# Order of two TensorE stages in the attention loop: weigh the values first, then turn the weights

## The chip, the core and the metric

One core of a Trainium2 chip runs the whole program. The metric is device time in microseconds (us) of one execution; lower is better. Engines are called TensorE (PE in the profile; PEld is its loading of stationary operands), VectorE (DVE), ScalarE (ACT), GpSimd (POOL) and SyncE (SP, which issues most transfers).

## The reference

One decoder layer: a half-step SwiGLU feed-forward block, a mixer of eight forgetting-attention heads (FoX) and eight native-sparse-attention heads (NSA), and a second feed-forward block, for 512 prompt tokens and eight samples of one token each. The part that matters here is the prompt's attention, cut down from the reference:

```python
# FoX heads
s = einsum('bqhd,bkhd->bhqk', q, k) * scale + cum[q] - cum[k]
s = where(kpos <= p, s, NEG)
a = softmax(s, axis=-1)
o = einsum('bhqk,bkhd->bqhd', a, v)
# NSA heads, selected branch and window branch (compressed branch apart)
a_slc, a_win = softmax(masked scores of each branch)
o = g_cmp * o_cmp + g_slc * (a_slc @ v_slc) + g_win * (a_win @ v_win)
```

With 512 tokens every 64-token block that lies before a query is selected, so both NSA branches are causal attention over all earlier keys.

## The kernel before

The feed-forward blocks and the projections (the three-product matmuls of line 1332) keep TensorE busy for most of the time and are not touched. Between them, from 561.8 to 699.6 us of the span, lies the prompt's attention, and behind it, to about 780 us, the attention of the eight samples and the output projection's start.

**Couples.** The attention loop goes over 48 *couples*. A couple is two heads at one block of 128 queries (`unit(v)` for v = 2m and 2m+1; couple m). The block number i = m mod 4 sets how many keys there are: 128·(i+1), so 128, 256, 384, 512 and again. Couples 0 to 15 are FoX heads; from 16 to 47 come the NSA heads, four couples of the selected branch and four of the window branch in turn. Below, *block 3* is a couple with i = 3, the widest.

**The stages of one couple, and who does them:**

- *Scores* (`scores`, lines 1459 to 1467, TensorE): QᵀK for both heads (64 rows of the array each), for FoX the forget sums (line 1465), and the causal mask (line 1467, a bf16 product). Scores of couple m wait for the exponentials of couple m − 2, whose banks they reuse.
- *Row max* (line 1081, VectorE), one instruction for both heads.
- *Exponentials* (line 792, ScalarE), one for each head, each followed by the reading of its accumulated row sum.
- *Scaling* by the reciprocal of the row sum and the gate (line 462), on GpSimd for blocks 0 and 1, on VectorE for blocks 2 and 3.
- *Turn* (`turn_p`, line 1476, TensorE): i+1 transposes for each head into PSUM bank 4 (even head) or 5 (odd head). It waits until that bank's last contents are drained.
- *Drain* (`turn_out`, line 481): VectorE copies the even head's bank, ScalarE the odd head's, into the tile PTS.
- *Weigh* (`weigh`, line 1492, TensorE): PTS times the values, 2(i+1) products of 64 columns, accumulated in bank 6 or 7. It waits for both drains of its couple.

**The order is written out by hand.** In step m TensorE does the scores of couple m, turns couple m − 3 and weighs couple m − 4, in the order that the change is about (function `attention` of the tensor block). Two other engines run the same steps in their own in-order queues. VectorE in step m: drain of couple m − 3 (even head), row max of couple m, reciprocals of couple m − 1, and where due its scaling:

```python
                    if m >= 3 and m != BURST_AT:
                        turn_out(dve, nc.vector.tensor_copy, 2 * (m - 3), "att_even_out")
                    if m < PAIRS:
                        v, W = 2 * m, P * (unit(2 * m)[3] + 1)
                        dve.wait_ge(sem("att_scored"), v + 2)
                        nc.vector.reduce_max(row_max[:, v:v + 2], ...
```

ScalarE in step m: drain of couple m − 3 (odd head), the two exponentials of couple m, and once for each pair of heads a copy of the finished output to OT (line 769). In step 14 (`BURST_AT`) TensorE also runs the 128 products of `windows` (line 1507) between its scores and the rest. Steps 48 to 51 have no scores: they only turn and weigh the last couples. SyncE and GpSimd wait for the last weigh before they start on the samples' part.

Of the kernel before, what the change touches and what calls it, by code (L numbers as in the profile page):

```python
# [122 lines left out]
def of_kind(j, kinds):  # L123

    return sum(t in kinds for t in TILES[:j])
# [7 lines left out]
def unit(v):  # L133

    if v < 4 * HF:
        return True, 2 * (v // 8) + v % 2, 0, v // 2 % 4, v // 8
    w = v - 4 * HF
    return False, 2 * (w // 16) + w % 2, w // 8 % 2, w // 2 % 4, 4 + w // 16
# [32 lines left out]
def layer_kernel(nc, I, O):  # L171
    with ExitStack() as ctx:
        made = {}

        def sem(name):
            if name not in made:
                made[name] = ctx.enter_context(nc.semaphore(name))
            return made[name]
# [1140 lines left out]
        def _(pe):  # L1319
# [130 lines left out]
            def scores(v):  # L1450

                fox, _, br, i, _ = unit(v)
                W = P * (i + 1)
                if v >= 4:
                    pe.wait_ge(sem("att_exp"), v - 2)
                for j in (0, 1):
                    h, part = unit(v + j)[1], slice(64 * j, 64 * j + 64)
                    q, k = (h // 2, h // 2) if fox else (4 + h // 2, 4 + 2 * br + h // 4)
                    nc.tensor.matmul(ps[:, score_bank(v + j), 0:W], QX[part, q, i * P:i * P + P], KX[part, k, 0:W],  # L1459
                                     start=True, stop=False, skip_group_check=True)  # L1460
                for j in (0, 1):
                    h, bank = unit(v + j)[1], ps[:, score_bank(v + j), :]
                    if fox:

                        nc.tensor.matmul(bank[:, 0:W], selb[:, h * P:h * P + P], cumb[:, 0:W],
                                         start=False, stop=False, skip_group_check=True)
                    nc.tensor.matmul(bank[:, W - P:W], identb[:, :], causalb[:, :], start=False, stop=True,  # L1467
                                     skip_group_check=True).then_inc(sem("att_scored"), 1)

            def turn_p(w):  # L1470
                i = unit(w)[3]
                pe.wait_ge(sem(scaled_by(w)), scaled_count(w))
                if w >= 2:
                    pe.wait_ge(sem("att_odd_out" if w % 2 else "att_even_out"), w // 2)
                for kb in range(i + 1):
                    q = nc.tensor.transpose(ps[:, 4 + w % 2, kb * P:kb * P + P],  # L1476
                                            weights(w)[:, kb * P:kb * P + P], ident)
                q.then_inc(sem("att_turned"), 1)

            def weigh(n):  # L1480

                pe.wait_ge(sem("att_even_out"), n + 1)
                pe.wait_ge(sem("att_odd_out"), n + 1)
                fox, _, br, i, t = unit(2 * n)
                first = br == 0 and i == 0
                if first and t >= 2:
                    pe.wait_ge(sem("att_out"), t - 1)
                for kb in range(i + 1):
                    for j in (0, 1):
                        h = unit(2 * n + j)[1]  # L1490
                        c = h * DH if fox else 512 + br * P + (h // 4) * DH
                        q = nc.tensor.matmul(ps[64 * j:64 * j + 64, 6 + t % 2, i * P:i * P + P], VT[:, kb, c:c + DH],  # L1492
                                             PTS[:, (2 * n + j) % PT_SLOTS, kb, :], start=first and kb == 0,
                                             stop=i == QT - 1 and kb == i and (fox or br == 1),
                                             skip_group_check=True)
                q.then_inc(sem("att_pv"), 1)

            def windows():

                for n in (0, 1):  # L1500
                    pe.wait_ge(sem(f"cmp_in{n}"), 16 * (3 + NPAGE))
                pe.wait_ge(sem("att_even_out"), BURST_AT - 3)
                pe.wait_ge(sem("att_odd_out"), BURST_AT - 3)
                for j in range(CMP_LEN):
                    for kv, n in ((0, 0), (1, 1), (0, 1), (1, 0)):
                        r, c = slice(64 * kv, 64 * kv + 64), slice(64 * n, 64 * n + 64)
                        q = nc.tensor.matmul(ps[c, 4 + kv, 0:N_WIN], W1[n][r, j, r],  # L1507
                                             view(X[n][r, :], j, [[CMP_STRIDE, N_WIN]]),
                                             start=j == 0, stop=j == CMP_LEN - 1, skip_group_check=True)
                q.then_inc(sem("cmp_hid"), 1)  # L1510

            def attention():
                for m in range(PAIRS + 4):
                    if m == 16:
                        pe.wait_ge(sem("stack_hi"), of_kind(NPROJ, STACKED))
                        pe.wait_ge(sem("stack_lo"), 2)
                    if m < PAIRS:
                        scores(2 * m)
                    if m == BURST_AT:
                        windows()  # L1520
                        pe.wait_ge(sem("hid_k_out"), 1)
                        pe.wait_ge(sem("hid_v_out"), 1)
                    if 3 <= m < PAIRS + 3:
                        turn_p(2 * (m - 3))
                        turn_p(2 * (m - 3) + 1)
                    if m >= 4:
                        weigh(m - 4)

            project()
            pe.wait_ge(sem("stack_hi"), of_kind(9, STACKED))  # L1530
# [2 lines left out]
            pe.wait_ge(sem("cum_ready"), 1)  # L1533
            pe.wait_ge(sem("bf_ready"), 1)
            attention()


# [277 lines left out]
```

## Time and profile before

| what | value |
|---|---|
| median of 3 runs | 1235.23 us (1234.47 to 1239.1) |
| the profiled execution | 1234.73 us, its span 1232.9 us |
| TensorE busy (PE), loading (PEld) | 1167.1 us (95%), 1078.0 us (87%) |
| VectorE, ScalarE, GpSimd busy | 534.2 us, 429.2 us, 136.0 us |
| chain that ended last, by engine | PE 87%, DVE 6%, ACT 3% |
| scores, L1459 | 192 products, 38.9 us busy |
| weigh, L1492 | 480 products, 36.8 us busy |
| row max, L1081 | 48 instructions, 39.1 us busy |

A row of the timeline reads: start, duration, engine, line, operation, output<-inputs, shapes, count; in square brackets how long the engine was idle before it, and what ended that. Runs of the same kind are merged into one row, so the time from the start of one row to the start of the next is what that stage took of TensorE, and the printed duration is longer by the last product's way through the array.

### The profile page before, as it was taken

How to read it: one execution, taken by the hardware profiler on the slowest of the kernel's cores; microseconds unless marked ns; L12 is line 12 of the kernel's file. 1: busy time of each engine (PE TensorE's matmuls, PEld its weight loads, DVE VectorE, ACT ScalarE, POOL GpSimd, SP SyncE). 2: the span in 40 equal slices, each digit the busy share in tenths (PEclk: the TensorE clock that was granted, in tenths of full speed). 3: DMA queues.
4: the chain of work that ended last, by engine and by line, in shares of the span. 5: the costliest groups of instructions: out<-in, count | busy, mean ns of one | idle time of the engine just before them, and what ended most of it. 6: DMA issues, size and time to landing. Idle time of an engine off the chain costs nothing.

```text
span 1232.9 us, 23635 instructions
## 1 busy us (share of the span) xinstructions
PE 1167.1 (95%) x9643; PEld 1078.0 (87%) x9650; DVE 534.2 (43%) x787; ACT 429.2 (35%) x740; POOL 136.0 (11%) x132
## 2 busy tenths in 40 slices
PE   9999999999999999998999756989999999999994
PEld 6999999999999799995666423979999999999994
DVE  4433432333333743455277646455343333333334
ACT  6222221222234542225266524454222221222332
POOL 0111100010111000223111100210011000011110
PEclk9999999999999999999999988999999999999998
DMA  6322223322223133217060062121232223222221
GB/s 273 103 75 95 86 78 111 103 84 87 78 87 111 54 121 135 90 62 236 20 205 2 7 185 103 68 69 47 91 102 80 69 100 114 83 102 89 66 86 70
DMA packets 46002, 117.95 MB, mean 96 GB/s; under 512 B 4154, under 2 KB 21818, under 8 KB 39874
## 3 DMA queue, kind: packets, MB, share of 16 engines
q1 hardware_dynamic: 42738, 110.95, 26.8%
q10 hardware_dynamic: 3184, 5.88, 1.2%
q8 instruction: 58, 0.95, 0.3%
q14 instruction: 22, 0.18, 0.0%
HBM read 110.93 MB, written 7.97 MB: 96 GB/s over the span
## 4 chain that ended last, share of the span: by engine, by line
PE 87%; DVE 6%; ACT 3%; issue 2%; DMA 1%; DVEq 0%; SPq 0%; ACTq 0%
PE ps L1332 75%; PE ps L1459 3%; PE ps L1476 2%; PE ps L1341 1%; PE ps L1507 1%; PE ps L1492 1%; DVE row_max L1081 1%; DVE UT L919 1%; DVE H L923 1%; DVE XL L899 1%; PE ps L1467 1%; ACT PRB L792 1%; PE ps L1425 0%; DMA RAW<-in_w_gu 0%; DMA KW<-in_win_k 0%
## 5 line engine op out<-in xcount | busy, mean ns | idle before, releaser
L1332 PE MATMUL ps<-XH,WH 128*128 128x260 f32 x1904 | 389.9, 286 | 8.0 <-DVE XL L899 7.9
L1332 PE MATMUL ps<-XH,WL 128*128 128x260 f32 x1904 | 383.7, 283 | 0.0
L1332 PE MATMUL ps<-XL,WH 128*128 128x260 f32 x1904 | 383.0, 283 | 0.0
L409 ACT CAST WH<-RAW 128x1024 fp32r<-128x1024 f32 (+2 forms) x183 | 174.8, 956 | 530.8 <-PE ps L1332 526.2
L1332 PEld LDWEIGHTS ps<-XH,WH 128*128 128x128 f32 x1904 | 295.2, 189 | 14.2 <-DVE XL L899 11.3
L1332 PEld LDWEIGHTS ps<-XH,WL 128*128 128x128 f32 x1904 | 293.7, 189 | 0.0
L1332 PEld LDWEIGHTS ps<-XL,WH 128*128 128x128 f32 x1904 | 293.1, 188 | 0.0
L412 DVE TENSOR_TENSOR WL<-RAW,WH 128x1024 fp32r<-128x1024 f32 (+2 forms) x183 | 203.7, 1113 | 157.9 <-ACT WH L409 156.7
L1332 PE MATMUL ps<-UL,WH 128*128 128x260 f32 x704 | 141.9, 283 | 0.0
L1332 PE MATMUL ps<-UH,WL 128*128 128x260 f32 x704 | 141.5, 282 | 0.0
L1332 PE MATMUL ps<-UH,WH 128*128 128x260 f32 x704 | 141.4, 282 | 0.0
L1277 POOL TENSOR_TENSOR UL<-HT,UH 128x520 f32 (+1 forms) x44 | 57.8, 1314 | 632.8 <-ACT UH L665 632.8
L1332 PEld LDWEIGHTS ps<-UH,WL 128*128 128x128 f32 x704 | 108.5, 188 | 0.0
L1332 PEld LDWEIGHTS ps<-UH,WH 128*128 128x128 f32 x704 | 108.4, 188 | 0.0
L1332 PEld LDWEIGHTS ps<-UL,WH 128*128 128x128 f32 x704 | 108.3, 188 | 0.0
L939 DVE TENSOR_TENSOR UT<-ps,token_rstd 128x520 f32<-128x520 f32 x44 | 30.8, 700 | 145.8 <-PE ps L1332 145.8
L935 DVE TENSOR_TENSOR GT<-ps,token_rstd 128x520 f32<-128x520 f32 x44 | 30.8, 700 | 128.7 <-PE ps L1332 119.9
L665 ACT CAST UH<-HT 128x520 f32 (+1 forms) x44 | 27.6, 627 | 86.0 <-DVE HT L946 86.0
L1052 DVE TENSOR_TENSOR TR<-ps,token_rstd 128x520 f32<-128x520 f32 x23 | 16.1, 700 | 67.9 <-PE ps L1332 44.8
L1459 PE MATMUL ps<-KX,QX 64*128 64x128 f32 (+3 forms) x192 | 38.9, 481 | 6.5 <-ACT PRB L792 5.1
L1081 DVE TENSOR_REDUCE row_max<-ps 128x2 f32<-128x256 f32 (+3 forms) x48 | 39.1, 815 | 6.7 <-PE ps L1467 6.7
L1270 POOL TENSOR_TENSOR ACC<-ACC,SQ 128x520 f32<-128x520 f32 x18 | 27.0, 1501 | 96.1 <-ACT SQ L613 96.1
(233 smaller groups left out, 927.4 us busy)
## 6 DMA issues: line engine op xcount, KB each, us to landing
RAW<-in_w_gu SPq DMA_DIRECT2D x44, 1024.0 KB, 4.8
RAW<-in_w_down SPq DMA_DIRECT2D x16, 768.0 KB, 4.7
RAW<-in_w_in SPq DMA_DIRECT2D x11, 1024.0 KB, 4.9
RAW<-in_w_down SPq DMA_DIRECT2D x16, 640.0 KB, 4.3
KF<-in_fox_k SPq DMA_DIRECT2D x16, 256.0 KB, 4.2
VF<-in_fox_v SPq DMA_DIRECT2D x16, 256.0 KB, 5.1
RAW<-in_w_out SPq DMA_DIRECT2D x4, 1024.0 KB, 4.9
H<-in_x SPq DMA_DIRECT2D x4, 520.0 KB, 7.2
```

Source lines behind the costliest of these rows:

```text
L409: nc.scalar.copy(WH[:, par, 0:width], RAW[:, slot, j, 0:width]).then_inc(w_hi, 1)
L412: nc.vector.tensor_tensor(WL[:, par, 0:width], RAW[:, slot, j, 0:width], WH[:, par, 0:width], ALU.subtract).then_inc(w_lo, 1)
L665: nc.scalar.copy(row(UH, st.m), HT[:, st.par, :]).then_inc(sem("hid_hi"), 1)
L935: nc.vector.tensor_tensor(two(GT[:, st.par, :]), halves(0), two(R1[:, :]), ALU.mult).then_inc(sem("evac"), 1)
L939: nc.vector.tensor_tensor(two(UT[:, st.par, :]), halves(1), two(R1[:, :]), ALU.mult).then_inc(sem("evac"), 1)
L1052: nc.vector.tensor_tensor(two(TR[:, j % 4, :]), halves(j % 2), two(R1[:, :]), ALU.mult).then_inc(sem("projected"), 1)
L1081: nc.vector.reduce_max(row_max[:, v:v + 2], ps[:, score_bank(v):score_bank(v) + 2, 0:W], AX.X, negate=True).then_inc(sem("att_max"), 1)
L1270: nc.gpsimd.tensor_tensor(ACC[:, :], ACC[:, :], SQ[:, par, :], ALU.add).then_inc(sem("acc"), 1)
L1277: nc.gpsimd.tensor_tensor(row(UL, st.m), HT[:, st.par, :], row(UH, st.m), ALU.subtract).then_inc(sem("hid_lo"), 1)
L1332: q = nc.tensor.matmul(ps[:, 2 * slot + half, 0:HALF], w[:, par, cols], x[:, kt0 + kt, half * HALF:(half + 1) * HALF], start=first and kt ...
L1459: nc.tensor.matmul(ps[:, score_bank(v + j), 0:W], QX[part, q, i * P:i * P + P], KX[part, k, 0:W], start=True, stop=False, skip_group_check ...
L1476: q = nc.tensor.transpose(ps[:, 4 + w % 2, kb * P:kb * P + P], weights(w)[:, kb * P:kb * P + P], ident)
```

## The change

In every step of the tensor block's attention loop the weigh of couple m − 4 is issued before the turns of couple m − 3, not behind them. Nothing else differs: the same instructions, waits and signals, on the other engines in the same order.

```diff
@@ -1520,11 +1520,11 @@
                         windows()
                         pe.wait_ge(sem("hid_k_out"), 1)
                         pe.wait_ge(sem("hid_v_out"), 1)
+                    if m >= 4:
+                        weigh(m - 4)
                     if 3 <= m < PAIRS + 3:
                         turn_p(2 * (m - 3))
                         turn_p(2 * (m - 3) + 1)
-                    if m >= 4:
-                        weigh(m - 4)
```

TensorE around a block-3 step, the two orders in one (L1459 and L1467 are scores, L1476 turns, L1492 weighs; a row's shape is its output):

```order
 L1459 MATMUL ps<-KX,QX 128x512 x2
 L1467 MATMUL ps<-causalb,identb 128x128 x2
+L1492 MATMUL ps<-PTS,VT 64x128 x8
 L1476 MATMUL ps<-consts,PRA 128x128 x2
-L1492 MATMUL ps<-PTS,VT 64x128 x8
 L1459 MATMUL ps<-KX,QX 128x128 x2
 L1467 MATMUL ps<-causalb,identb 128x128 x2
+L1492 MATMUL ps<-PTS,VT 64x128 x2
 L1476 MATMUL ps<-consts,PRA 128x128 x4
-L1492 MATMUL ps<-PTS,VT 64x128 x2
```

The weigh now stands directly behind the scores, and the turns directly ahead of the next scores.

TensorE at the loop's end, from the scores of couple 47 (steps 47 to 51), again both in one:

```order
 L1459 MATMUL ps<-KX,QX 128x512 x2
 L1467 MATMUL ps<-causalb,identb 128x128 x2
+L1492 MATMUL ps<-PTS,VT 64x128 x8
 L1476 MATMUL ps<-consts,PRA 128x128 x2
+L1492 MATMUL ps<-PTS,VT 64x128 x2
+L1476 MATMUL ps<-consts,PRA 128x128 x4
+L1492 MATMUL ps<-PTS,VT 64x128 x4
+L1476 MATMUL ps<-consts,PRB 128x128 x6
+L1492 MATMUL ps<-PTS,VT 64x128 x6
+L1476 MATMUL ps<-consts,PRB 128x128 x8
 L1492 MATMUL ps<-PTS,VT 64x128 x8
-L1476 MATMUL ps<-consts,PRA 128x128 x4
-L1492 MATMUL ps<-PTS,VT 64x128 x2
-L1476 MATMUL ps<-consts,PRB 128x128 x6
-L1492 MATMUL ps<-PTS,VT 64x128 x4
```

Here each weigh now follows at once on the turns of its own couple; before, the turns of the next couple stood between them.

VectorE in the block-3 step and the one behind it, the same before and after the change:

```order
L481 COPY PTS<-ps 128x128
L1081 TENSOR_REDUCE row_max<-ps 128x2
L1086 RECIPROCAL row_inv<-row_sum 128x2
L462 TENSOR_SCALAR PRB<-PRB,row_inv,gates 128x384 x2
L481 COPY PTS<-ps 128x256
L1081 TENSOR_REDUCE row_max<-ps 128x2
```

The drain of the couple turned in a step (L481) stands ahead of the row max (L1081) of the couple scored in that step.

## Rows read from the trace of the kernel before

**Rows 1.** Busy time in two stretches (columns PE, PEld, DVE, ACT, POOL, PEclk, DMA share, GB/s).

```profile
613.60:699.60 86.00, 81.28 (x775) 52.87 (x776) 62.71 (x152) 53.66 (x175) 15.91 (x32) 1.00 0.25 81
560.00:570.00 10.00, 7.53 (x54) 4.07 (x55) 4.67 (x11) 6.27 (x19) 3.39 (x5) 1.00 0.89 316
```

**Rows 2.** Timeline of TensorE over four steps, scores of block 3 first.

```profile
653.13 1.13 PE L1459 MATMUL ps<-KX,QX 64*128 64x512 f32 x4
654.20 0.29 PE L1467 MATMUL ps<-causalb,identb 128*128 128x128 bf16 x2
654.32 0.39 PE L1476 MATMUL ps<-consts,PRA 128*128 128x128 f32 x2
654.64 1.09 PE L1492 MATMUL ps<-PTS,VT 128*64 128x128 f32 x16
655.66 0.49 PE L1459 MATMUL ps<-KX,QX 64*128 64x128 f32 x4
...
657.59 0.70 PE L1459 MATMUL ps<-KX,QX 64*128 64x256 f32 x4 [0.41 <-ACT PRB L792]
...
658.35 0.82 PE L1476 MATMUL ps<-consts,PRB 128*128 128x128 f32 x6
659.10 0.66 PE L1492 MATMUL ps<-PTS,VT 128*64 128x128 f32 x8
659.69 0.92 PE L1459 MATMUL ps<-KX,QX 64*128 64x384 f32 x4
...
660.66 1.04 PE L1476 MATMUL ps<-consts,PRB 128*128 128x128 f32 x8
661.64 0.88 PE L1492 MATMUL ps<-PTS,VT 128*64 128x128 f32 x12
662.44 1.13 PE L1459 MATMUL ps<-KX,QX 64*128 64x512 f32 x4
...
664.97 0.49 PE L1459 MATMUL ps<-KX,QX 64*128 64x128 f32 x4
```

**Rows 3.** Timeline of the same stretch, VectorE and ScalarE.

```profile
654.64 0.29 DVE L481 COPY PTS<-ps 128x128 f32<-128x128 f32 x1 [1.01 <-PE ps L1476]
...
654.84 1.21 DVE L1081 TENSOR_REDUCE row_max<-ps 128x2 f32<-128x1024 f32 x1
...
656.09 0.69 ACT L792 ACTIVATE PRB<-ps,row_max 128x512 f32<-128x512 f32 x1 [1.08 <-DVE row_max L1081]
...
657.34 0.20 ACT L792 ACTIVATION_READ_ACCUMULATOR PRB<-ps,row_max 128x1 f32 x1
...
663.93 0.20 ACT L792 ACTIVATION_READ_ACCUMULATOR PRB<-ps,row_max 128x1 f32 x1
```

**Rows 4.** Waits from 560 to 725 us: total us, times, longest.

```profile
PE ps L1459 <- ACT PRB L792: 5.1, 12, 0.8
```

**Rows 5.** Timeline, scores of couple 0 to scores of couple 1.

```profile
562.45 0.22 PE L1467 MATMUL ps<-causalb,identb 128*128 128x128 bf16 x1
562.60 0.70 PE L1459 MATMUL ps<-KX,QX 64*128 64x256 f32 x4
```

**Rows 6.** Timeline of the loop's end.

```profile
694.66 0.37 ACT L481 COPY PTS<-ps 128x256 f32<-128x256 f32 x1
...
694.74 0.95 PE L1476 MATMUL ps<-consts,PRB 128*128 128x128 f32 x6 [0.83 <-DVE PTS L481]
...
695.73 0.48 ACT L481 COPY PTS<-ps 128x384 f32<-128x384 f32 x1 [0.70 <-PE ps L1476]
...
696.62 1.06 PE L1476 MATMUL ps<-consts,PRB 128*128 128x128 f32 x8 [0.33 <-DVE PTS L481]
...
697.72 0.59 ACT L481 COPY PTS<-ps 128x512 f32<-128x512 f32 x1 [1.51 <-PE ps L1476]
...
699.58 0.59 ACT L769 COPY OT<-ps 128x512 f32<-128x512 f32 x1 [1.27 <-PE ps L1492]
```

## The prediction

> **What bounds the kernel now.** I read the busy time by stretch first. From 613.6 us to the loop's end TensorE is busy 81.28 of 86 us at a granted clock of 1.00, VectorE, the next, 62.71 of 86 [rows 1]. So time on TensorE is time of the kernel, and the question is what TensorE waits for. The table of waits names one thing inside the loop: scores wait for the exponentials of a wide couple, 12 times, 5.1 us in all [rows 4]. The timeline of four steps shows where: only the scores of a block-1 couple stop, by 0.41 us, and what releases them is the exponential (PRB, L792) of the block-3 couple two steps earlier [rows 2]. The other three steps of the four run without a stop.
>
> That wait ends a chain that I follow with the third view [rows 2, 3]. Scores of block 3 start at 653.13, the turns behind them at 654.32. VectorE drains the even head at 654.64 as soon as its turn is there, having been idle for 1.01 us, and only then, at 654.84, takes the row max of the scores, which had been ready since about 654.49 (654.20 + 0.29). The row max lasts 1.21 us, the exponentials run from 656.09 to 657.54 (657.34 + 0.20), and the scores of couple m + 2 start at 657.59. The chain takes 657.59 - 653.13 = 4.46 us; TensorE's own work in the same two steps is 4.46 - 0.41 = 4.05 us. **The reader should see one thing in these rows:** the row max stands behind the drain in VectorE's queue, the drain waits for the turn, and so the turn is on the chain while the weigh, which comes after it, is not. TensorE's products run beside VectorE's row max.
>
> **The change, part by part.** Nothing is added or removed; in each step that has both, the weigh moves ahead of the turns; 44 of these steps have scores too. No transfer and no instruction of another queue moves.
>
> *The block-3 step.* With the weigh between scores and turns, the drain starts later by the whole weigh, and with it row max, exponentials and the scores of couple m + 2. The weigh of a block-3 couple takes 654.64 to 655.66 = 1.02 us of TensorE [rows 2]. Since the scores already wait there, nothing absorbs it.
>
> *What a switch costs.* The products of a stage start on one another closely, but where the shape of the loaded operand changes there is a step. From the masks of the scores to the turns, both 128 by 128, two masks and the switch take 654.20 to 654.32, 0.06 us for each mask [rows 2]. From the last mask to the next scores, 64 rows instead of 128, it is 562.45 to 562.60 = 0.15 us [rows 5]. The new switch from masks to a weigh (64 columns) is in no row of the loop. I bound it by these two: 0.00 to 0.09 us more than the switch that it replaces, and I take 0.09, since the weigh is a change of shape too. The other two switches, weigh to turns and turns to scores, take the place of weigh to scores and turns to weigh, all four with a change of shape, so I put their difference at nothing.
>
> The chain becomes 4.46 + 1.02 + 0.09 = 5.57 us, TensorE's work in it 4.05 + 0.18 = 4.23 us, the wait 1.34 us in place of 0.41. It is paid for the block-3 couples 7, 11, ..., 43, which is 10 times (couple 3 has no weigh in its step, couple 47 belongs to the end): 10 x 1.11 = **11.1 us**.
>
> *The Trainium skill on this switch.* "TensorE: Matmul & The Clock Gate", section "Step-by-step: what each phase is for", says that the engine can pull the loading of the next operand ahead of products in flight. By that the weigh's first load hides behind the masks, the 0.09 is 0, and the sum is the 1247.0 worked out under the rivals; the pair of rows that I go by speaks against it for a change of rows, and no row shows it for a change of columns.
>
> *The other steps.* Blocks 1 and 2 stay bound by TensorE and pay only the switch. Of the 44 steps 20 lie in the ten chains, step 47 in the end, step 4 disappears in a wait, step 14 has the compression products between scores and weigh: 21 x 0.09 = **1.9 us**. Do their chains have room? The nearest is block 2: scores start at 659.69, exponentials end at 664.13 (663.93 + 0.20), the scores that need them start at 664.97, so 0.84 us are left [rows 2, 3]. The weigh of block 2 adds 0.80 (661.64 to 662.44) and a switch 0.09, and TensorE itself comes 0.18 later: 0.84 - 0.89 + 0.18 = 0.13 us are left. Just enough, so I cost it at nothing; if this cover fails it is paid ten times.
>
> *The loop's end.* Behind the last scores each weigh now waits for ScalarE's drain of turns issued just before it. Couple 45's drain ends at 695.03 (694.66 + 0.37); it stands behind the exponentials of couple 47, whose chain is 1.11 longer, so 696.14, and the weigh starts at 696.19. From there, with stage lengths from the rows: weigh 45 0.59 (659.10 to 659.69), turns 46 0.75 (658.35 to 659.10), a wait, weigh 46 0.80, turns 47 0.98 (660.66 to 661.64), a wait, weigh 47 1.02 [rows 2]. A wait is ScalarE's drain, 0.48 and 0.59, and 0.16 around it (0.07 until the turn's printed end, 0.04 and 0.05 for the two signals): 0.64 and 0.75 [rows 6]. In sum 701.72, and with 0.11 until the last product is out 701.83, against 699.58 now: **2.2 us**. The two waits that turns have there today, 0.83 and 0.33, are already inside the 699.58.
>
> *Sum.* 11.1 + 1.9 + 2.2 = 15.2 us. Everything behind the loop waits for its last weigh and moves as a whole. On the profiled execution: 1234.73 + 15.2 = 1249.9, rounded to **1250**; that execution lies 0.5 us below the median of the three runs, far less than 0.5% of the time (6.2 us), which is about what a measurement of this kernel can tell from no change.
>
> **The rivals.**
>
> *The switch is free* (0.20). Chain and end alone: 10 x 1.02 + 2.1 = 12.3, so 1247.0. For it: masks to turns shows none. Against it: the change of shape.
>
> *The block-2 chain binds too, or a scaling comes late* (0.10). The 0.13 us of room is a difference of larger numbers. If drains or scalings cost 0.1 to 0.4 more than I think, ten periods pay 1 to 4 us: 1251 to 1254.
>
> *Turns gain what scores lose, and the kernel is faster* (0.02). A turn waits until its bank is drained; behind the weigh the drain has more time. If the scores' wait were made by the turns and not by the row max behind the drain, all 5.1 us of it [rows 4] and the 0.83 + 0.33 at the end [rows 6] could go: 1234.7 - 6.3 = 1228.4. It decides itself at the drain: were VectorE busy until the turn is done, the row max would lose nothing. Against it: VectorE was idle 1.01 us ahead of that drain [rows 3]. The skill's "Perfetto Trace Analysis", section "Matmuls", asks that groups rotate through banks so that copying one out overlaps the next group's products. By that rule the new order is the better one, with the weigh between two uses of the turn's banks; the trace shows no wait for these banks inside the four steps, so the rule has nothing to win there.
>
> *The extra delay is hidden* (0.05). If the exponentials had other work to wait for, only the end and the switches would stay, 0 to 4 us: 1235 to 1239. Against it: ScalarE was idle for 1.08 us until the row max came [rows 3].
>
> *The granted clock falls to the lower of its two levels* (0.03), because TensorE now waits more: its 8.9 us of work in four steps would take about twice as long, 8.9 us for each time: 1259 and more. Against it: from 560 to 570 us TensorE was busy only 7.53 of 10 us at a granted clock of 1.00 [rows 1], and the new loop would be about 87% busy.
>
> **How the numbers follow.** The forecast has 0.60 and gives 1250. The range takes in the free switch (1247.0) and the binding block 2 (1254), and 1 to 2 us at either side for the runs: 1245 to 1255. Outside lie the last three rivals, together 0.10, and the tails of the others, so about 0.15. Faster by over 0.5%: 0.02. Within 0.5% (1229 to 1241.4): 0.05. Slower by over 0.5%: 0.93.
>
> **What would show it.** Right, step by step: scores of block 1 wait 1.2 to 1.4 us for the exponential of block 3, where it was 0.41; four steps of NSA heads take 10.6 us where they take 9.31 (653.13 to 662.44); the weigh starts 0.15 us behind the last mask (0.06 if the switch is free); row max of block 3 starts 1.1 us later after its scores; in the loop's end weighs wait for drains and turns do not; behind the loop all is as it was. Wrong: scores of block 1 with a wait of 0.4 us or none, a wait at the scores of block 0, or a granted clock under 1.00 before 700 us.

## The result, and the profile after

The changed kernel takes 1261.26 us (median of 4 executions, 1259.64 to 1264.59) where the kernel before, on the same chips, took 1237.16 us: a ratio of 1.020, 95% interval 1.018 to 1.022. A second measurement later in the study gave 1261.75 against 1236.94 us, ratio 1.020, interval 1.018 to 1.022. So the change costs 24 to 25 us. It was forecast to be slower, but by 15 us, and the time lies above the range.

The page of the profiled execution (1264.59 us, span 1262.7 us) shows the same work in a longer span. Its first part gives busy time, its second the granted clock in 40 slices, in tenths of full speed:

```profile
PE 1186.0 (94%) x9643; PEld 1087.8 (86%) x9650; DVE 533.1 (42%) x787; ACT 430.0 (34%) x740; POOL 136.0 (11%) x132
...
PEclk9999999999999899999999867999999999999997
```

VectorE and ScalarE do as much as before. TensorE is busy 19 us longer with the same products. About 6 us of that are the dearer switches between stages that the experiments price (44 steps at 0.145 us, an estimate from their rows); the rest are products that ran slower: the mean granted clock is 0.966, where it was 0.983.

Four steps of NSA heads on TensorE, answering to [rows 2]; the columns are those of that group:

```profile
654.67 1.13 PE L1459 MATMUL ps<-KX,QX 64*128 64x512 f32 x4
655.74 0.29 PE L1467 MATMUL ps<-causalb,identb 128*128 128x128 bf16 x2
655.95 1.09 PE L1492 MATMUL ps<-PTS,VT 128*64 128x128 f32 x16
656.98 0.44 PE L1476 MATMUL ps<-consts,PRA 128*128 128x128 f32 x2
657.34 0.49 PE L1459 MATMUL ps<-KX,QX 64*128 64x128 f32 x4
...
660.30 0.70 PE L1459 MATMUL ps<-KX,QX 64*128 64x256 f32 x4 [1.29 <-ACT PRB L792]
...
665.43 1.13 PE L1459 MATMUL ps<-KX,QX 64*128 64x512 f32 x4
```

From block 3 to block 3 it is 10.76 us instead of 9.31, and the scores of block 1 wait 1.29 us instead of 0.41. VectorE and ScalarE in the same stretch, answering to [rows 3]:

```profile
657.34 0.29 DVE L481 COPY PTS<-ps 128x128 f32<-128x128 f32 x1 [1.37 <-PE ps L1476]
...
657.55 1.22 DVE L1081 TENSOR_REDUCE row_max<-ps 128x2 f32<-128x1024 f32 x1
...
658.80 0.69 ACT L792 ACTIVATE PRB<-ps,row_max 128x512 f32<-128x512 f32 x1 [1.08 <-PE ps L1476]
...
660.05 0.20 ACT L792 ACTIVATION_READ_ACCUMULATOR PRB<-ps,row_max 128x1 f32 x1
```

The scores of block 3 start at 654.67 and the row max at 657.55, 2.88 us later; it was 1.71 (653.13 to 654.84). The drain in front of the row max came 1.17 us later because its turn stood behind the weigh. That is the forecast mechanism, and 1.1 was the forecast size.

What was not in the forecast is the granted clock. Busy time by stretch (PE, PEld, DVE, ACT, POOL, then PEclk), three stretches inside the loop and two around its end:

```profile
671.00:681.80 10.80, 9.47 (x84) 5.87 (x84) 7.00 (x17) 6.07 (x22) 1.99 (x4) 1.00 0.00 0
681.80:685.20 3.40, 3.38 (x20) 2.30 (x20) 1.50 (x5) 1.45 (x6) 0.00 (x0) 0.57 0.03 7
685.20:696.00 10.80, 9.51 (x85) 5.85 (x84) 6.65 (x16) 6.03 (x20) 1.99 (x4) 0.98 0.00 0
704.80:716.00 11.20, 8.96 (x80) 5.58 (x81) 7.15 (x18) 6.75 (x22) 1.99 (x4) 1.00 0.01 1
716.00:726.00 10.00, 7.55 (x50) 5.84 (x50) 4.72 (x25) 2.03 (x4) 0.96 (x2) 0.52 0.00 1
```

From 681.8 to 685.2 us, in the middle of the loop, the mean granted clock is 0.57: most of this stretch lies at the lower of TensorE's two levels (1.2 instead of 2.4 GHz). From 716 us on it is there again. Before the first of these it had been waiting 1.29 us of every 10.76; before the second it had waited 0.45 and 1.77 us for two drains. The loop's end on TensorE, answering to [rows 6]:

```profile
713.15 0.44 PE L1492 MATMUL ps<-PTS,VT 128*64 128x128 f32 x4 [0.45 <-ACT PTS L481]
...
715.94 0.72 PE L1492 MATMUL ps<-PTS,VT 128*64 128x128 f32 x8 [1.77 <-ACT PTS L481]
...
718.79 1.55 PE L1492 MATMUL ps<-PTS,VT 128*64 128x128 f32 x12 [0.66 <-ACT PTS L481]
...
723.01 1.97 PE L1492 MATMUL ps<-PTS,VT 128*64 128x128 f32 x16 [0.77 <-ACT PTS L481]
...
725.02 0.59 ACT L769 COPY OT<-ps 128x512 f32<-128x512 f32 x1 [2.15 <-PE ps L1492]
```

The waits are the forecast ones (0.66 and 0.77 for couples 46 and 47; 0.64 and 0.75 were worked out), but the weighs at 718.79 and 723.01 run at half speed, 1.55 and 1.97 us for what takes 0.88 and 1.09.

Where the time went in one profiled execution of each kernel. The program is cut at the first and the last scores, at the last copy to OT (L769) and at the output projection's first product; us:

```
                        until    first to   to the    to the    rest   mean
                        first    last       last      output           granted
                        scores   scores     OT copy   proj.            clock
before                  561.85   128.51      9.22     69.38    463.94  0.983
changed                 563.70   146.26     15.06     73.79    463.89  0.966
changed, again          561.82   148.03     11.90     74.27    463.88  0.970
old order at the end    562.78   146.51     11.44     73.80    463.87  0.970
new order, block 3      560.62   142.93     10.39     69.38    463.98  0.982
new order, not block 3  562.77   131.85      9.21     70.22    463.95  0.980
changed, idle products  562.46   146.30     11.90     70.16    463.98  0.979
changed, row max first  561.67   131.13     10.71     72.16    463.83  0.979
before, row max first   560.83   127.60      8.90     69.33    463.94  0.982
new order at the end    561.79   128.82     10.73     74.21    463.85  0.974
before, long delay      561.02   149.69     12.99     71.87    463.93  0.973
before, short delay     560.98   141.72     11.41     74.16    463.93  0.973
before, both first      561.07   137.57      9.49     73.80    463.87  0.975
```

The first column is the same code in all of them, so its 3 us of spread are not the change's.

One thing in this table needs care: the only profile of the kernel before is of one of its faster executions. Its 25 executions in the second measurement fall into two groups, 13 at 1233.9 to 1236.9 us with a granted clock of 0.980 to 0.984, and 12 at 1238.0 to 1240.3 us with 0.974 to 0.979.

### The profile page after: what moved, and what is told of

It is laid out like the page before. It is cut to its first block, busy times and chain, and to the rows that moved or that the text cites. A ratio compares the mean times of both kernels' runs of the same rounds, so it can differ in the third digit from the quotient of the medians.

```text
span 1262.7 us, 23635 instructions
## 1 busy us (share of the span) xinstructions
PE 1186.0 (94%) x9643; PEld 1087.8 (86%) x9650; DVE 533.1 (42%) x787; ACT 430.0 (34%) x740; POOL 136.0 (11%) x132
## 4 chain that ended last, share of the span: by engine, by line
PE 89%; DVE 5%; ACT 3%; issue 2%; DMA 1%; DVEq 0%; SPq 0%; ACTq 0%
PE ps L1332 74%; PE ps L1459 3%; PE ps L1492 3%; PE ps L1476 3%; PE ps L1341 2%; PE ps L1507 1%; DVE UT L919 1%; ACT PRB L792 1%; DVE H L923 1%; PE ps L1467 1%; DVE XL L899 1%; DMA RAW<-in_w_gu 1%; PE ps L1634 0%; PE ps L1425 0%; DMA KW<-in_win_k 0%
## 5 line engine op out<-in xcount | busy, mean ns | idle before, releaser
L1459 PE MATMUL ps<-KX,QX 64*128 64x128 f32 (+3 forms) x192 | 40.3, 497 | 15.2 <-ACT PRB L792 13.8
L481 DVE COPY PTS<-ps 128x128 f32<-128x128 f32 (+3 forms) x48 | 23.5, 489 | 52.3 <-PE ps L1476 52.3
L1492 PE MATMUL ps<-PTS,VT 128*64 128x128 f32 x480 | 38.9, 294 | 4.5 <-ACT PTS L481 3.6
```

The lines of the kernel that those rows point to most:

```text
L481: copy(PTS[:, w % PT_SLOTS, 0:i + 1, :], ps[:, 4 + w % 2, 0:P * (i + 1)].rearrange("p (a n) -> p a n", n=P)).then_inc(sem(name), 1)
```

## The experiments

Each edit is against the kernel before, unless it says otherwise; where only the line with `weigh_first` is shown, the other lines are those of the first edit. Two theories. **The queue:** TensorE waits longer because the drain stands ahead of the row max on VectorE, and the granted clock falls because TensorE waits. **The order itself:** the changes of operand shape, or the weighs' own waits, make the cost, and the clock falls for the new order or by chance. "m" is the step; PAIRS is 48.

### The end in the old order

```diff
+                    weigh_first = m < PAIRS
-                    if m >= 4:
+                    if m >= 4 and weigh_first:
                         weigh(m - 4)
                     if 3 <= m < PAIRS + 3:
                         turn_p(2 * (m - 3))
                         turn_p(2 * (m - 3) + 1)
+                    if m >= 4 and not weigh_first:
+                        weigh(m - 4)
```

> The new order in steps 4 to 47, the old one in steps 48 to 51. If the chain through the row max makes the loop's cost and the waits of the last weighs make the rest (directly, and through the lower granted clock behind them), this is 15 to 18 us over the kernel before, the clock behind the loop is as before (about 0.8), and the stretch from the last weigh to the output projection's first product is back at 69 to 71 us. If the clock falls because of the waits inside the loop, little changes: 21 to 24 us over, and that stretch stays at 73 to 74 us.

Measured: 1259.61 us against 1238.41, ratio 1.017, interval 1.014 to 1.021, so 21 us over. The clock is 0.970 and the stretch to the output projection stays at 73.80 us. It is the second case: against the changed kernel the old end saves 2 to 4 us (by the medians, or by the differences to the kernel before), and the clock does not need the waits of the last weighs to fall.

### The new order in the block-3 steps alone

```diff
+                    weigh_first = m < PAIRS and m % 4 == 3
```

> The new order only in the steps that score a block-3 couple (one of four). Chain theory: scores of block 1 wait about 1.3 us and four steps take 1.1 to 1.2 us more than before, 11 to 13 us in all. If instead the changes of operand shape in every step make the cost, only a quarter of it is here: 3 to 5 us in all, and the wait stays near 0.4 us.

Measured: 1250.40 us against 1238.41, ratio 1.012, interval 1.008 to 1.015: 12 us. On TensorE:

```profile
646.34 0.70 PE L1459 MATMUL ps<-KX,QX 64*128 64x256 f32 x4 [1.43 <-ACT PRB L792]
...
652.25 0.28 PE L1467 MATMUL ps<-causalb,identb 128*128 128x128 bf16 x2
652.46 1.09 PE L1492 MATMUL ps<-PTS,VT 128*64 128x128 f32 x16
653.49 0.44 PE L1476 MATMUL ps<-consts,PRA 128*128 128x128 f32 x2
653.86 0.49 PE L1459 MATMUL ps<-KX,QX 64*128 64x128 f32 x4
...
656.81 0.70 PE L1459 MATMUL ps<-KX,QX 64*128 64x256 f32 x4 [1.43 <-ACT PRB L792]
```

Four steps take 10.47 us, 1.16 more than before, from one step of four. The chain holds. The rows also give the switches: masks to weigh 0.21 us (652.25 to 652.46) where masks to turns were 0.12, so 0.09 dearer, as taken; weigh to turns 1.03 for 1.02; but from the first turn to the next scores 0.37 (653.49 to 653.86) where from the first turn to the weigh it was 0.32. That 0.05 had been put at nothing. Where it arises, single rows show. The kernel before (PE products, PEld loads):

```profile
654.26 0.22 PE L1467 MATMUL ps<-causalb,identb 128*128 128x128 bf16 x1
654.26 0.20 PEld L1476 LDWEIGHTS ps<-consts,PRA 128*128 128x128 f32 x2
654.43 0.27 PE L1476 MATMUL ps<-consts,PRA 128*128 128x128 f32 x1
```

The changed kernel:

```profile
655.80 0.22 PE L1467 MATMUL ps<-causalb,identb 128*128 128x128 bf16 x1
655.95 0.85 PEld L1492 LDWEIGHTS ps<-PTS,VT 128*64 128x64 f32 x16
656.98 0.33 PE L1476 MATMUL ps<-consts,PRA 128*128 128x128 f32 x1
657.14 0.27 PE L1476 MATMUL ps<-consts,PRA 128*128 128x128 f32 x1
```

The second turn starts 0.16 us behind the first (656.98 to 657.14), where it was 0.11 (654.32 [rows 2] to 654.43). From the second turn to what follows it is the same, 0.20 (657.14 to 657.34) and 0.21 (654.43 to 654.64). So the 0.05 lies in the first turn, which now stands behind a stage of another shape, and it is on the chain: 1.02 + 0.09 + 0.05 = 1.16.

### The new order everywhere but in the block-3 steps

```diff
+                    weigh_first = m < PAIRS and m % 4 != 3
```

> The new order in all steps with scores but those of block 3. Chain theory: the three short chains have room, so only the switches are paid, 1 to 4 us over the kernel before, and the wait of the block-1 scores stays at 0.4 us or less. If every weigh ahead of a turn is on a chain, 6 us or more.

Measured: 1239.44 us against 1238.41, ratio 1.002, interval 1.000 to 1.004. Three quarters of the change cost 1 us by the medians (the interval allows 0 to 4), and 3.3 us of loop in the profile:

```profile
646.65 1.13 PE L1459 MATMUL ps<-KX,QX 64*128 64x512 f32 x4
...
651.11 0.70 PE L1459 MATMUL ps<-KX,QX 64*128 64x256 f32 x4 [0.24 <-ACT PRB L792]
...
656.25 1.13 PE L1459 MATMUL ps<-KX,QX 64*128 64x512 f32 x4
```

Four steps take 9.60 us, 0.29 more than before, and 0.29 + 1.16 is the whole 1.45 of the changed kernel. The two parts add up.

### Idle products in the waits of the end

Added to the changed kernel:

```diff
+WARM_END = {49: 8, 50: 3, 51: 3}
...
                     if m >= 4:
+                        if m in WARM_END:
+                            pe.wait_ge(sem("att_exp"), 94)
+                            keep_warm(WARM_END[m], bank=0)
                         weigh(m - 4)
```

> The changed kernel with 14 idle products (512 columns, bf16, result never read) put into the waits of the last three weighs, 8, 3 and 3 of them, 0.2 us each at the full clock. If the lower granted clock in the last turns and weighs comes from TensorE standing still there, those stages run at 1.00, the loop's end takes 11 to 12 us instead of 15, and the kernel is 4 to 8 us faster than the changed one. If the clock falls for another reason, the products only add: no faster, or 1 to 3 us slower than the changed kernel.

Measured: 1260.21 us against 1238.41, ratio 1.019, interval 1.016 to 1.023, about 1 us less than the changed kernel and far from 4 to 8. The end took 11.90 us, as expected, but in the changed kernel's second profile it took 11.90 too, without the products. The stretch behind it was 70.16 us in this profile, where it was 73.79 and 74.27; with a median as high as it is, that can't be put down to the products. The attempt failed. In this profile two stretches at the lower level lie inside the loop, at 636 and 681 us, ahead of these products, which can do nothing about them.

### The changed kernel with the row max ahead of the drain

```diff
                 for m in range(PAIRS + 3):
-                    if m >= 3 and m != BURST_AT:
-                        turn_out(dve, nc.vector.tensor_copy, 2 * (m - 3), "att_even_out")
                     if m < PAIRS:
...
                                              negate=True).then_inc(sem("att_max"), 1)
+                    if m >= 3 and m != BURST_AT:
+                        turn_out(dve, nc.vector.tensor_copy, 2 * (m - 3), "att_even_out")
```

> The changed kernel with VectorE's queue turned round in each step: row max first, then the drain. If the cost comes over the drain that stands ahead of the row max, the weigh is off the chain again, the scores of block 1 wait 0.2 us or less, four steps take 9.5 to 9.8 us, the granted clock is as in the kernel before, and the whole is 3 to 7 us over it. If the cost lies in the order on TensorE itself (switches of shape, waits for the drains), it stays 15 us or more over.

Measured: 1241.22 us against 1236.94, ratio 1.004, interval 1.002 to 1.005: 4 us over. TensorE's order is the changed one, instruction by instruction, and 20 of the 24 us are gone:

```profile
649.34 0.70 PE L1459 MATMUL ps<-KX,QX 64*128 64x256 f32 x4
...
654.48 1.13 PE L1459 MATMUL ps<-KX,QX 64*128 64x512 f32 x4
...
658.92 0.70 PE L1459 MATMUL ps<-KX,QX 64*128 64x256 f32 x4
```

The scores of block 1 are down to 0.11 us of idle time (the views print only what is over 0.15), four steps take 9.58 us, and no stretch of the loop is at the lower level. This decides for the queue. What is left in the loop is the switches: 9.58 against the 9.00 of the next kernel, where the same queue meets the old order, is 4 times 0.145 us.

### The kernel before with the row max ahead of the drain

The same edit of VectorE's queue, made to the kernel before.

> The kernel before with the same turn in VectorE's queue, the order of TensorE as it was. Chain theory: the 0.41 us wait of the block-1 scores, 11 times, goes to under 0.1 us and the loop is 3 to 4.5 us shorter, so 3 to 4 us faster than the kernel before. If drains that now come later stop the turns or the weighs, no gain or a loss of 1 to 3 us.

Measured: 1232.36 us (8 executions, 1230.59 to 1234.52) against 1236.94, ratio 0.9964, interval 0.9949 to 0.9979. **It beats both kernels**, by 4.6 and 29 us. The block-3 step there, all three engines:

```profile
653.51 0.28 PE L1467 MATMUL ps<-causalb,identb 128*128 128x128 bf16 x2
653.63 0.39 PE L1476 MATMUL ps<-consts,PRA 128*128 128x128 f32 x2
653.84 1.22 DVE L1079 TENSOR_REDUCE row_max<-ps 128x2 f32<-128x1024 f32 x1 [1.34 <-PE ps L1467]
...
654.98 0.28 DVE L481 COPY PTS<-ps 128x128 f32<-128x128 f32 x1
...
655.09 0.69 ACT L792 ACTIVATE PRB<-ps,row_max 128x512 f32<-128x512 f32 x1 [0.77 <-DVE row_max L1079]
```

The row max now starts 0.33 us behind the start of the masks (653.51 to 653.84) and no longer waits for the turn. In the same timeline TensorE is idle for 0.10 us ahead of the scores of block 1, where it was 0.41, so this chain has almost gone; four steps take 9.00 us (647.60 to 656.60 in the same timeline). The drain comes later and holds nobody up inside the loop.

### The new order at the end alone

```diff
+                    weigh_first = m >= PAIRS
```

> The new order in steps 48 to 51 only. The loop is as before; its end takes about 1.1 us longer at the full clock. If the longer waits there are enough to bring the granted clock down, the turns and weighs behind them take about 3 us more and the stretch to the output projection 3 to 4 more: 6 to 8 us over the kernel before. If the waits inside the loop are needed for that too, 1 to 3 us over.

Measured: 1240.66 us against 1236.94, ratio 1.003, interval 1.001 to 1.004: 3.7 us, between the two cases. The end takes 10.73 us, 1.5 more than before (1.1 was worked out). In the profile the stretch behind it takes 74.21 us instead of 69.38, but the clock of its ten executions, 0.971 to 0.979, overlaps that of the kernel before (0.974 to 0.984 in the 25 executions beside it). But not one of the ten lies in the upper group, 0.980 and more, where 13 of those 25 do. So a few waits at the end can cost some clock, 2 us by the medians, but not the 7 us in question.

### The changed kernel again

> The changed kernel once more, beside the others on one chip. If the lower granted clock is part of the change and not of one execution, its share is again 0.966 to 0.975, with stretches at the lower level inside the loop, at its end and behind it, and the time is 22 to 25 us over the kernel before; if it was chance, 16 to 18 us over at a clock of 0.98.

Measured: 1261.75 us (1260.79 to 1262.59), 24.8 us over, with a granted clock of 0.969 to 0.972 in all four executions. The lower clock belongs to the change. In this profile the loop has three stretches at the lower level (at 625, 659 and 703 us), in the first it had two (at 566 and 682 us), and the loop was 1.8 us longer.

### A delay in place of the new order

TensorE keeps its old order; VectorE does further row maxes whose results nobody reads, ahead of the real one (`unread` is a new tile). The short delay has WIDTHS = (512,).

```diff
+WIDTHS = (512, 128)
...
                         dve.wait_ge(sem("att_scored"), v + 2)
+                        if m >= 4 and m % 4 == 3:
+                            for e, n in enumerate(WIDTHS):
+                                c = 4 * (m // 4) + 2 * e
+                                nc.vector.reduce_max(unread[:, c:c + 2],
+                                                     ps[:, score_bank(v):score_bank(v) + 2, 0:n], AX.X,
+                                                     negate=True)
```

> TensorE in its old order; the block-3 row max is made later by two further row maxes of the same scores (512 and 128 columns), whose results nobody reads. The chain grows by about 1.13 + 0.34 = 1.47 us, as much as four steps of the changed kernel take more, so that TensorE waits 1.9 us for each block-1 scores: 11 x 1.47 = 16 us from the waits. If waits alone bring the granted clock down inside the loop, as in the changed kernel, its share is 0.970 to 0.976 and the kernel is 20 to 24 us over the one before; if the new order of TensorE is needed for that, the clock stays at 0.98 and it is 15 to 18 us over.

Measured: 1261.12 us against 1239.05, ratio 1.018, interval 1.016 to 1.020: 22 us, with a clock of 0.969 to 0.974. Four steps at the full clock took 10.76 us, to the hundredth what the changed kernel takes. In the timeline (lines are shifted by 8 in this kernel, so L1467 is scores) and by stretch:

```profile
670.47 0.70 PE L1467 MATMUL ps<-KX,QX 64*128 64x256 f32 x4 [1.87 <-ACT PRB L794]
...
673.21 1.65 PE L1467 MATMUL ps<-KX,QX 64*128 64x384 f32 x4
...
682.76 0.70 PE L1467 MATMUL ps<-KX,QX 64*128 64x256 f32 x4 [1.87 <-ACT PRB L794]
```

```profile
670.50:677.00 6.50, 6.50 (x48) 4.10 (x50) 3.67 (x9) 3.00 (x11) 0.88 (x2) 0.74 0.01 1
677.00:681.00 4.00, 3.89 (x38) 2.26 (x38) 2.99 (x6) 1.42 (x5) 1.09 (x2) 1.00 0.02 4
```

Behind a wait of 1.87 us the scores of block 2 take 1.65 us instead of 0.92, and this period lasts 12.29. The old order on TensorE, with nothing but longer waits, gives the same time and the same clock as the changed kernel. So the waits bring the clock down, not the new order. The added work on VectorE is no rival for that: it is busy 549.0 us here, but 533.1 in the changed kernel, as before.

> The same with the wide further row max alone: the chain grows by 1.13 us, as it did where only the block-3 steps had the new order. 11 x 1.13 = 12.4 us over the kernel before, four steps of NSA heads in 10.4 us, no lower clock inside the loop.

Measured: 1254.39 us against 1239.05, ratio 1.012, interval 1.010 to 1.015: 15 us, where 12.4 was expected. Four steps took 10.44 us as worked out (645.65 to 656.09 in its timeline), but there was one stretch at the lower level inside the loop, and the clock was 0.971 to 0.977.

### Exponentials ahead of the drain as well

On top of the row max first, ScalarE does both exponentials of couple m before the drain of couple m − 3:

```diff
-                    if m >= 3 and m != BURST_AT:
-                        turn_out(act, nc.scalar.copy, 2 * (m - 3) + 1, "att_odd_out")
                     if m < PAIRS:
                         act.wait_ge(sem("att_max"), m + 1)
...
                                 sem("att_exp"), 1)
+                    if m >= 3 and m != BURST_AT:
+                        turn_out(act, nc.scalar.copy, 2 * (m - 3) + 1, "att_odd_out")
```

> The kernel before with row max ahead of the drain on VectorE and both exponentials ahead of the drain on ScalarE. The chain through the row max is as short as it gets, but ScalarE's drain of couple m - 3 comes 1 us and more later, and the odd head's next turn waits for it: where the wait of the block-1 scores has gone, waits of the odd turns after block-3 and block-2 exponentials come in its place. 0 to 8 us slower than the kernel with the row max alone moved; if nothing waits for those drains it is the same within 1 us.

Measured: 1248.26 us against 1239.05, ratio 1.008, interval 1.006 to 1.010. It is 14 to 16 us slower than the row max alone (by the differences to the kernel before, or by the medians), about twice what was allowed for. The wait has moved:

```profile
652.88 0.26 ACT L481 COPY PTS<-ps 128x128 f32<-128x128 f32 x1
...
653.29 0.41 PE L1476 MATMUL ps<-consts,PRA 128*128 128x128 f32 x2 [0.93 <-ACT PTS L481]
```

The drain of the block-0 couple now stands behind both exponentials of block 3, and the odd head's next turn waits 0.93 us for it. Four steps take 9.96 us (644.04 to 654.00). The same trade that pays on VectorE loses on ScalarE, whose work between turn and drain is longer.

## Why the prediction was wrong

**The bound and the chain: right.** The row max behind the drain behind the turn was named as the chain, and the weigh as what would be put on it. The block-3 steps alone cost 1.16 us for four steps (1.11 was worked out), three quarters of the change cost next to nothing, and with the row max moved ahead of the drain the cost went, TensorE's order unchanged. That is shown by runs on both sides: the order without the cost, and the cost (by a delay) without the order.

**The switches: mis-sized, 0.145 for 0.09.** Masks to weigh cost 0.09 more, as taken from the pair of rows on a change of rows; the rival of a free switch (0.20) falls. The Trainium skill, "TensorE: Matmul & The Clock Gate", section "Step-by-step: what each phase is for", says that the engine can pull a load ahead of products in flight, under conditions. The trace agrees for the turns in the kernel before, whose first load starts with the last mask (654.26 and 654.26), and not for the weigh in the changed kernel, whose first load starts 0.15 us behind the last mask (655.95 and 655.80). What the prediction left out is that the first turn behind the weigh is 0.05 us slower; the other switches differ by nothing in their starts, as it had put them. So a step pays 0.145 (0.58 for four steps) where 0.09 was counted. Masks, turns and weighs differ in more than the shape of the loaded operand, and no run separates the shape from the rest. At the full clock the ten periods cost 14.5 us (10.76 - 9.31 = 1.45 each) and the loop, with two more dear switches in its last steps, about 14.8; the prediction had 11.1 + 1.9 = 13.0.

**The cover of block 2: right.** Its 0.13 us of room held. No scores of block 0 waited.

**The loop's end: mechanism right, size a little small.** 11.90 - 9.22 = 2.7 us at the full clock; 2.2 was worked out.

**The granted clock: this step failed.** The prediction's sum has the clock at nothing, for the loop and for what follows; it gave a fall of the clock 0.03, and wrote that everything behind the loop "moves as a whole". Its own sign of being wrong, a granted clock under 1.00 before 700 us, came (0.57 from 681.8 us). At the full clock the change costs 14.8 + 2.7 = 17.5 us, which on top of the 1235 us of before would have been about 1253, inside the range; the measured 24 to 25 need another 7. In the second profile they can be counted: 1261.82 - 1234.73 = 27.1 us, of which 17.5 are waits and switches, 4.7 are three stretches at the lower level inside the loop (148.03 - 128.51 - 14.8), and 4.9 the samples' part (74.27 for 69.38). The last may not be all the change's: 4 to 5 us is also the distance between the two groups of executions of the kernel before, and this comparison takes its faster one. That the slower group is the one with the longer samples' part is likely, but not shown, since none of it was profiled. The argument against it had been one row: TensorE busy 7.53 of 10 us at a clock of 1.00 [rows 1]. That row shows that a single such stretch can pass, not that all of a longer, more broken loop will. It did not even hold for itself: in the changed kernel's first profile the lower level comes at 566 us, in steps that the change does not touch, and the profiles of two other kernels (new order in block 3; before, row max first) have it from 560 us on. The price in that rival, 8.9 us for each period, was wrong too: one stretch of 3.4 us at half the clock costs 1.5 to 1.6 us (12.29 for 10.76 in the long delay; 146.26 - 128.51 - 14.8 = 2.95 for two). So its "1259 and more" came about by luck: from short stretches on top of switches and an end that cost more than forecast, not from a period at half the clock.

**The rivals.** Faster (0.02) and hidden (0.05) are out. The faster one had a true core, though: the queue's order on VectorE was worth 4.6 us, by a different edit.

**What stays open.** Why one stretch falls to the lower level and its like does not. The new order in the block-3 steps alone has waits of 1.43 us in periods of 10.47 and none of it inside the steady loop in its profile; the short delay, with 1.54 in 10.44, has one; 1.29 in 10.76 has one to three in four profiles, and 1.87 in 10.76 has four. The kernels with waits of 0.41 us or less at these scores, the one before and four others, have none in the loop (one of them has it across the loop's first steps), nor has the kernel with 0.93 us at the odd turns, but for its first steps. More waiting made it more frequent, but this rests on one profile of each kernel, two of the changed one. Nor is it settled why the samples' part takes 69.4 us in some kernels and 74 in others with the same code; the kernel before itself ranges over 6 us, in two groups.

## What to carry to other kernels

When two stages on the busiest engine are exchanged, look at the in-order queues of the engines that serve them: here a drain stood ahead of the row max on VectorE, so whatever was put ahead of a turn was put ahead of the next exponentials. Where a chain of waits is already seen in the trace, 0.4 us long and repeated, the cheap repair is to let the instruction on the chain go first in that queue (0.4% here), and to check that what goes second has nobody waiting. And where a change lengthens regular waits of TensorE by a few per cent, add the clock to the sum: here it was about 7 of 24 us.

## What the runs showed of the hardware

TensorE can fall to the lower of its two levels inside a loop in which it is busy for about 90% of the time by the profile (22.42 of 25 us from 640 to 665 us in the changed kernel, 24.18 in the one before): two or three stretches of 3.4 us, each costing 1.5 to 1.6 us. One more switch between stages with operands of different shapes costs 0.145 us of TensorE: 0.09 until the weigh starts behind the masks, and 0.05 in the first turn behind the weigh. Neither was in the prediction's sum at its full size.
